# Attention heads in two batches of four, V's product on column halves, retention scores in one visit

## The reference, cut to what matters

```
h = rmsnorm(x, pre_mix_norm);  proj = h @ w_in        # 256 tokens, 1024 -> 3072 columns
rq, rk, rv, rg, mq, mk, mv = split(proj)
# retention, 4 heads, q/k of 64, v of 128, two chunks of 128 tokens, rotary on q and k
scores = (qi @ ki.T) * decay;  o = scores @ vi + decayed state   # then per-head RMS norm, silu(rg) gate
# attention, 8 heads of 64; with 256 tokens there is one block, so it is plain causal softmax + T5 bias
p = softmax(q @ k.T / 8 + bias[bucket(i - j)], causal);  o = p @ v
mix = concat([ret, moba]) @ w_out;  x = x + rmsnorm(mix, post_mix_norm)
f = (silu(h @ w_gate) * (h @ w_up)) @ w_down           # h = rmsnorm(x, pre_ffn_norm), 2816 hidden
x = x + rmsnorm(f, post_ffn_norm)
```

## Time and profile before

| | |
|---|---|
| median of 3 runs | 310.75 us (310.51 to 311.15) |
| the profiled execution | 310.8 us, of which the span of the trace is 308.9 us |
| DVE busy | 187.8 us (61%) |
| ACT busy | 154.0 us (50%) |
| POOL busy | 14.1 us (5%) |

### The profile page before, as it was taken

How to read it: one execution, slowest core, us unless ns; L and a number is a source line. 1 busy time by engine, 2 the same in 40 slices (tenths; PEclk the granted TensorE clock), 3 DMA queues, 4 the chain that set the end, 5 groups by cost and what they waited for, 6 DMA issues and landing times.

```text
span 308.9 us, 4097 instructions
## 1 busy us (share of the span) xinstructions
PE 302.2 (98%) x1408; PEld 245.7 (80%) x1408; DVE 187.8 (61%) x281; ACT 154.0 (50%) x253; POOL 14.1 (5%) x24
## 2 busy tenths in 40 slices
PE   8999999999999999999999999999999999999992
PEld 3888877788888888887888888888888888888881
DVE  2866567797589588978645554635446464542146
ACT  4989364466337445585536344435254363540231
POOL 1030100000011004100000000000000000000001
PEclk9999999999999999999999999999999999999998
DMA  6999985308333580559946465474745464500003
GB/s 190 406 406 382 411 347 168 137 2 268 138 135 85 190 271 4 159 207 344 341 168 187 162 210 198 146 259 138 256 142 208 150 198 158 211 36 0 0 0 136
DMA packets 17544, 58.33 MB, mean 189 GB/s; under 512 B 2003, under 2 KB 2556, under 8 KB 17532
## 3 DMA queue, kind: packets, MB, share of 16 engines
q1 hardware_dynamic: 17136, 57.06, 52.8%
q0 software_dynamic: 304, 1.06, 1.0%
q10 hardware_dynamic: 92, 0.05, 0.1%
HBM read 57.10 MB, written 1.06 MB: 188 GB/s over the span
## 4 chain that ended last, share of the span: by engine, by line
PE 90%; DVE 6%; ACT 1%; issue 1%; DVEq 0%; POOL 0%; ACTq 0%
PE bank L976 25%; PE bank L978 25%; PE bank L977 25%; PE bank L986 4%; DVE w_lo L885 3%; PE bank L1009 1%; PE bank L993 1%; PE bank L1096 1%; PE bank L1013 1%; PE bank L1017 1%; PE bank L1080 1%; DVE d_lo L892 1%; DVE res L967 1%; ACT junk L467 1%; DVE res L961 1%
## 5 line engine op out<-in xcount | busy, mean ns | idle before, releaser
L976 PE MATMUL bank<-w_hi,a_hi 128*128 128x512 f32 x256 | 101.5, 397 | 0.0
L978 PE MATMUL bank<-w_hi,a_lo 128*128 128x512 f32 x256 | 100.0, 391 | 0.0
L977 PE MATMUL bank<-w_lo,a_hi 128*128 128x512 f32 x256 | 99.6, 389 | 0.0
L978 PEld LDWEIGHTS bank<-w_hi,a_lo 128*128 128x128 f32 x256 | 48.0, 188 | 10.4
L976 PEld LDWEIGHTS bank<-w_hi,a_hi 128*128 128x128 f32 x256 | 48.1, 188 | 10.0 <-issue 0.7
L977 PEld LDWEIGHTS bank<-w_lo,a_hi 128*128 128x128 f32 x256 | 48.1, 188 | 9.6
L885 DVE TENSOR_TENSOR w_lo<-raw,w_hi 128x1024 fp32r<-128x1024 f32 x40 | 48.1, 1243 | 7.9 <-ACT w_hi L608 7.9
L692 DVE TENSOR_TENSOR w_lo<-raw,w_hi 128x1024 fp32r<-128x1024 f32 x32 | 38.1, 1220 | 9.1 <-ACT w_hi L458 9.1
L623 ACT ACTIVATE sil<-bank,rstd 128x256 f32<-128x256 f32 x22 | 10.4, 474 | 62.2 <-PE bank L978 60.1
L608 ACT ACTIVATE w_hi<-raw 128x1024 fp32r<-128x1024 f32 x40 | 40.1, 1053 | 0.0
L900 DVE SCALAR_TENSOR_TENSOR hid<-bank,rstd,sil 128x256 f32<-128x256 f32 x22 | 10.6, 482 | 46.3 <-ACT sil L623 46.3
(11 more groups left out here) (114 smaller groups left out, 282.1 us busy)
## 6 DMA issues: line engine op xcount, KB each, us to landing
raw<-in_w_gu SPq DMA_DIRECT2D x44, 512.0 KB, 4.4
raw<-in_w_dn SPq DMA_DIRECT2D x22, 512.0 KB, 4.1
raw<-in_w_in SPq DMA_DIRECT2D x20, 512.0 KB, 8.3
raw<-in_w_out SPq DMA_DIRECT2D x8, 512.0 KB, 3.3
raw<-in_w_in SPq DMA_DIRECT2D x8, 256.0 KB, 5.8
xs<-in_x SPq DMA_DIRECT2D x2, 512.0 KB, 8.5
bias<-bias_row POOLq DMA_DIRECT2D x1, 1024.0 KB, 10.1
out<-res SPq DMA_DIRECT2D x4, 256.0 KB, 2.0
```

The costliest lines, as they stand in the source:

```text
L976: pe.matmul(acc, hi, wh, start=first, stop=False)
L977: pe.matmul(acc, hi, wl, start=False, stop=False)
L978: return pe.matmul(acc, lo, wh, start=False, stop=last)
```

## The change

Constants: `FOURS` replaces `PAIR_U`, `RS_U` replaces `RS_SLOT`. Scores are now made for four heads at once, behind units 10 and 14, two of them in `wk` and two in the pair of `pj` that is free at that time. Transposes stay in four visits of two heads (behind units 12, 13, 16, 17). ACT instead of DVE copies the transposed probabilities to `pT`, which now has four buffers. V's product is made for four heads at once behind units 14 and 18: a head's 64 columns of `v` (no zeros) are the stationary operand on one half of the array's columns, the odd head's on the other half. Retention scores run on row halves, all four heads behind unit 20, two in `wk` and two in `po`; `rqk` takes the place of `rk` and `rqz`, and no zeros are written. ACT empties `po` in turns 15 and 19, ahead of that turn's exponentials; DVE's `m_lo` moves to turns 19 and 20.

```diff
-LO_UNITS = {16: [], 17: [], 18: [20, 21], 19: [22, 23]}
+LO_UNITS = {15: [], 16: [], 17: [], 18: [19, 20, 21], 19: [22, 23]}
...
-RS_SLOT = {20: [0, 1], 21: [2, 3]}
+RS_U = 20
-PAIR_U = [10, 12, 14, 16]
-EVAC = [17, 21]
-EVAC_LO = [20, 21]
+FOURS = [10, 14]
+EVAC = [15, 19]
+EVAC_LO = [19, 20]
...
+        def score_bank(h):
+            n, j = divmod(h, 4)
+            return (pj[1 - n] if j < 2 else wk)[:, j % 2, :]
+        def turn_bank(h):
+            return [wk[:, 0, :], wk[:, 1, :], po[:, 1, :], wk[:, 0, :]][h % 4]
...
-                pool.memset(vz[:, :, :, odd, 1 - odd, :], 0.0).then_inc(vz_zeroed, 1)
-                pool.memset(rqz[rows, odd:RH:2, :], 0.0).then_inc(rqz_zeroed, 1)
... ScalarE
+                        act.activation(pT[:, h % 4, :], turn_bank(h)[:, 0:3 * P], ACT.Copy).then_inc(pT_ready, 1)
...
+                    rows_out(v, 2, r_x, v_nat)
...
+                        act.activation(rqk[:, 0:RH, toks], src, ACT.Copy).then_inc(rT_ready, 1)
... VectorE
-                    dve.tensor_copy(pT[:, h % 2, :], wk[:, h % 2, 0:3 * P]).then_inc(pT_ready, 1)
... TensorE
+                if u - 4 in FOURS:
+                    n = FOURS.index(u - 4)
+                    if n == 0:
+                        pe.wait_ge(v_nat, NT)
+                    pe.wait_ge(pT_ready, 4 * n + 4)
+                    for b in (2 * n, 2 * n + 1):
+                        for t in range(NT):
+                            for odd in range(2):
+                                rows = slice(64 * odd, 64 * odd + 64)
+                                h = 2 * b + odd
+                                ins = pe.matmul(po[rows, n, b % 2 * S + t * P:(b % 2 + 1) * S],
+                                                v[:, t, h * MD:(h + 1) * MD], pT[:, h % 4, 2 * t * P:(t + 2) * P],
+                                                start=(t == 0), stop=(t == 1))
...
+                if u == RS_U:
+                    pe.wait_ge(rT_ready, NT)
+                    pe.wait_ge(pT_ready, MH)
+                    for b in range(RH // 2):
+                        if b == 1:
+                            pe.wait_ge(ahead_lo, 2)
+                        for t, toks in enumerate([slice(0, S), slice(P, S)]):
+                            for odd in range(2):
+                                rows = slice(64 * odd, 64 * odd + 64)
+                                ins = pe.matmul([wk, po][b][:, odd, 2 * t * P:(2 + t) * P],
+                                                rqk[rows, RH // 2 + b, tile(t)], rqk[rows, b, toks],
+                                                start=True, stop=True)
```

More of the change, by code:

```diff
@@ L129, in hybrid_layer @@
                 rot = sb("rot", [P, NT, CW], scope=late)
-                rk = sb("rk", [P, RH // 2, S], scope=late)
-                rqz = sb("rqz", [P, RH, S], scope=late)
+                rqk = sb("rqk", [P, RH + RH // 2, S], scope=late)
                 rs = sb("rs", [P, RH, 3 * P], scope=late)
@@ L508, in _ @@
             for u in range(N_IN):
-                for h in (u - 1 - S0, u - S0) if u - 1 in PAIR_U else ():
+                if u in EVAC:
+                    j = EVAC.index(u)
+                    act.wait_ge(pv_done, 4 * j + 4)
+                    act.activation(turned_heads(m_hi, j), backwards(po_heads(j)), ACT.Copy
+                                   ).then_inc(ahead_hi, 1)
+                for h in range(u - 1 - S0, u + 3 - S0) if u - 1 in FOURS else ():
                     act.wait_ge(l_ready, h + 1)
@@ L751, in _ @@
                                     ).then_inc(kT_odd, 1)
-                if u - 1 in PAIR_U:
+                if u - 1 in FOURS:
                     if u == S0 + 1:
                         dve.wait_ge(bias_loaded, 16)
[L755 to L760, removed]
-                    dve.tensor_copy(pT[:, h % 2, :], wk[:, h % 2, 0:3 * P]).then_inc(pT_ready, 1)
+                    for h in range(u - 1 - S0, u + 3 - S0):
+                        logits(h)
+                scaled_heads = ((u - 1 - S0, u - S0) if u - 1 in FOURS else
+                                (u - S0, u + 1 - S0) if u - 2 in FOURS else ())
+                for h in scaled_heads:
+                    dve.wait_ge(p_ready, NT * (h + 1))
+                    small(dve.reciprocal(erec[:, :, h:h + 1], esum[:, :, h:h + 1]))
+                    for t, (a, b) in enumerate([(0, P), (P, 3 * P)]):
+                        dve.tensor_scalar(pr[:, h % 4, a:b], pr[:, h % 4, a:b], erec[:, t, h:h + 1], None,
+                                          ALU.mult).then_inc(pn_ready, 1)
                 if u == 4 * UPG:
@@ L766, in _ @@
                     rotary(1)
[L767 to L774, removed]
+                if u <= RS_U:
                     for n in LO_UNITS.get(u, [u + LEAD]):
@@ L782, in _ @@
                                       ).then_inc(nq_ready, 1)
-                for h in RS_SLOT.get(u - 1, []):
+                for h in range(RH) if u == RS_U + 1 else ():
                     if h == 0:
@@ L1066, in _ @@
                         turn(wk[:, t, :], kn[:, t, :], MB, k_turned)
-                if u in PAIR_U:
-                    b = PAIR_U.index(u)
-                    if b == 0:
-                        pe.wait_ge(kT_ready, 1)
-                        pe.wait_ge(kT_odd, 1)
-                    else:
-                        pe.wait_ge(l_ready, 2 * b)
-                    if b > 1:
-                        pe.wait_ge(pT_ready, 2 * b - 2)
-                    for t, keys in enumerate([slice(0, P), slice(0, S)]):
-                        cols = slice(t * P, (2 * t + 1) * P)
-                        for odd in range(2):
-                            rows = slice(64 * odd, 64 * odd + 64)
-                            ins = pe.matmul(wk[:, odd, cols], qT[rows, b, tile(t)], kT[rows, b, keys],
-                                            start=True, stop=True)
-                            if t == 1:
-                                ins.then_inc(s_done, 1)
```

99 lines of the change are left out of this document (40 added, 59 removed).

## The result

The changed kernel takes 306.42 us (median of 4 runs, 306.12 to 306.56) against 310.66 us for the kernel before: ratio 0.986, 95% interval 0.985 to 0.9875. The forecast was 306.8 us. The profiled execution took 306.56 us, of which the span is 304.8 us.

What follows compares the result with a forecast made beforehand. TensorE's stream was taken to bound the kernel; gains of 1.00 (scores), 1.80 (V's product), 0.90 (retention scores) and 0.25 us (restarts) sum to 3.95 us, giving 306.8 us from 310.75, range 306.0 to 309.5.

Steps and rivals of the forecast that it cites:

- What bounds the kernel: TensorE's stream: a microsecond leaving it is one of the kernel if other engines stay ahead; relief elsewhere is worth nothing.
- Scores: Four visits of two heads become two of two row-half pairs: 4.40 us to 3.40, gain 1.00 us.
- V's product: Eight heads in series become four side-by-side column-half pairs in two visits: 5.20 us to 3.40, gain 1.80 us.
- Retention scores: Four heads in two visits become two row-half pairs and one switch: 2.60 us to 1.70, gain 0.90 us.
- Restarts: Three slow first product steps, 0.31 us instead of 0.23, go behind units 14, 16 and 20: gain 0.25 us.
- The sum: Gains on TensorE from scores, V's product, retention scores and restarts: 3.95 us.
- The other engines: Hand-overs to TensorE stay in time: least slack 1.9 us in the first batch, 2.0 us at `ahead_lo` in the second.
- Slack at `ahead_lo`: TensorE's new wait before the second retention pair, behind unit 20: second `m_lo` done 2.0 us before it is due.
- The rival of a new wait: DVE 3 us behind in the second batch, 1 us showing at `ahead_lo` or unit 19: 307.9 us, chance 0.05.
- Serial column halves: Rival: V's column halves run one behind the other, 2.60 us back, 309.4 us; chance 0.13.
- Exposed weight loads: Rival: column halves' weight loads are not hidden, V's passes cost 11.2 us, kernel slower at 315.4 us; chance 0.06.
- No gain: Rival: packing gains nothing, V serial and switches dearer than 0.40 us, 310 to 311 us; chance 0.04.

Runs made afterwards that it cites:

- e1_one_half: Changed kernel, but V's product of all eight heads on the same half of the array's columns, head after head (output wrong): 309.24 us.
- e3_ret_one_half: Changed kernel, but odd heads' retention scores read the same rows 0 to 63 as the even heads (output wrong): 307.89 us.
- e6_score_pairs: Changed kernel, but scores of four heads split into two visits of one pair each, behind units 10 and 11 and 14 and 15: 307.28 us.
- e8_pt_dve: Changed kernel, but VectorE instead of ScalarE makes the eight copies to `pT`, as in the kernel before: 306.46 us.
- e5_v_alone: Changed kernel, but V's product of the first four heads stands behind unit 15 instead of directly behind unit 14's scores: 306.70 us.
- e9_late1: Changed kernel, but VectorE's low part of unit 24 made twice, each time waited for, about 1.3 us more on VectorE: 306.68 us.
- e10_late3: Changed kernel, but VectorE's low part of unit 24 made four times, each waited for, about 3.9 us more on VectorE: 309.07 us.
- e4_ret_two: Changed kernel, but retention scores in two visits, two heads behind unit 20 and two behind unit 21, on row halves: 307.11 us.
- e2_turns: Changed kernel, but in each pair of V's product the even head's two matmuls are issued before the odd head's: 306.67 us.
- e11_far: Changed kernel, but V's product issues all four matmuls of the even column half, then all four of the odd half: 307.72 us.

## Why the prediction was right

- *What bounds the kernel.* TensorE's stream, and nothing given back later: shown. The projection starts 4.24 us earlier and the kernel is 4.24 us faster by the medians; a microsecond put back on TensorE's stream came back as a microsecond of time (e1_one_half, e3_ret_one_half, e6_score_pairs), and work moved between DVE and ACT came back as nothing (e8_pt_dve).
- *Scores*, gain of 1.00 us: right. The visit behind unit 10 costs 1.71 us, 1.70 forecast, and the gain is entries and exits (0.39 and 0.4 us each when put back) plus the wait that is gone.
- *V's product*, forecast 1.80 us: the mechanism is right, since putting the two heads on one half costs 2.6 us. The term was sized too low by 0.35 us. The switch into and out of column halves was priced at the 0.40 us of row halves and measured 0.30 behind unit 18 (1.60 - 1.30), where transposes follow, and 0.35 with a product behind it (1.65 - 1.30, e5_v_alone); and the visit behind unit 14 saved 0.25 us of the 0.80 charged for two switches.
- *Retention scores*, gain of 0.90 us: right (1.71 for 1.70 us).
- *Restarts*, gain of 0.25 us: wrong, this term should have been nothing. The prediction charged 0.08 us a visit because the first product step takes 0.31 us in place of 0.23. But the same rows show that this product starts 0.57 us behind the last head's first matmul (79.83 to 80.40) and not 0.65, so the time is only moved from one step to the next, and where scores precede, their 1.05 us hold the slow step already. The whole visit behind unit 16 of the kernel before costs 2.82 - 0.46 = 2.36 us, which is 1.05 for the scores and 1.30 for V, with nothing on top:

```profile
60.74 0.39 PE L978 MATMUL bank<-w_hi,a_lo 128*128 128x512 f32 x1
...
63.56 0.39 PE L977 MATMUL bank<-w_lo,a_hi 128*128 128x512 f32 x1
```

- *The sum.* 12.20 us of visits became 8.17, 4.03 us, where 3.95 was forecast: V's product was too low and the restarts too high by nearly as much, and that the sum came out so close is partly luck. The trace shows 4.24 us. Of the 0.2 us between, 0.15 lie in plain product steps, which take 0.2294 us on average before and 0.2283 after, over some 135 of them; why is not shown. So the forecast of 306.8 missed 306.42 by 0.3 us of gain and by 0.1 us at its base (310.75 in place of 310.66).
- *The other engines.* Slack at `ahead_lo` forecast 2.0 us, 1.7 in the trace, confirmed from both sides by e9_late1 (1.3 us hidden) and e10_late3 (a delay of 3.8 us, 2.05 of it seen). VectorE was 0.4 us earlier than reckoned and TensorE 0.6 us. The rival of a new wait names the right place, but no wait came.
- *The rivals.* Serial column halves: excluded by the 1.52 us of a group against 2.81. Exposed weight loads: excluded, and the loads became shorter. No gain: excluded.

What stays open: why plain product steps differ by a thousandth of a microsecond between traces (the 0.06 us that e4_ret_two has beyond its visits lie there too, at 0.2287 a step), and the one run of e9_late1 at 310.3 us, whose mean clock of 0.998 leaves no room for a stretch like that of e10_late3.

## What to carry to other kernels

Where TensorE is 98% busy with no waits, price a change from start-to-start differences in its timeline, and check that the other engines arrive by listing when each hand-over is due; here the one slack that was tested, worked out, was right within 0.3 us. Price a visit by its whole window, from the last product ahead of it to the second behind it, and not by single steps added on top. Two small matmuls on opposite halves of the rows or of the columns cost as much as one; what remains is getting into and out of the split, so put all packed work of a kind into as few visits as the PSUM banks allow, and let visits with different splits follow each other directly (worth 0.1 to 0.2 us each here). Keep the two halves' instructions close together in the program order.

## What the runs showed of the hardware

- Column halves of float32 matmuls stream fully side by side, each with all 128 rows: 1.52 us on alternate halves against 2.81 us on one half for the same 16 passes.
- Entry and exit cost 0.40 us around row halves, and around column halves 0.35 us ahead of a product and 0.30 us ahead of transposes; a change from row to column halves inside a visit costs 0.20 us less than two separate visits, and one from column to row halves 0.14 us less.
- TensorE lets a half run ahead of the order of issue by four passes (e2_turns, 0.05 us lost), not by eight (e11_far, 0.70 us lost), so matmuls on different halves need not start in the order of issue.
- An idle stretch of 1.89 us of TensorE was followed in the profiled execution by 3.5 us at the lower clock, which made it cost 3.7 us in place of 2.1. Five of the ten executions of this kernel had a mean clock (0.998 or above) that leaves no room for this.
- The first 512-column product behind retention scores on the whole array shows a step of 0.31 us in place of 0.23, but starts 0.08 us early, so nothing is lost by it.
